# Two MoE layers: rounds of experts in another order, and the weight ring planned in that order of use

## What is computed

```python
def moe(h2, router_w, router_b, w1, w3, w2):
    scores = sigmoid(h2 @ router_w)                    # 256 tokens x 16 experts
    # best of 4 groups by biased scores, then the best 2 experts in it
    gates = sel / sum(sel)
    ...
    for each expert e, xb = the tokens that chose it:
        y = (silu(xb @ w1[e]) * (xb @ w3[e])) @ w2[e]  # 1024 -> 512 -> 1024
        out[tokens] += y * gate
```

## Time and profile before

| what | value |
|---|---|
| median of three runs | 1976.16 us |
| the profiled execution: its own time | 1980.94 us |
| its span, from first to last instruction | 1979.1 us |
| mean granted clock of TensorE | 0.943 of full |
| PE busy | 1756.6 us (89%) |
| DVE busy | 975.3 us (49%) |
| ACT busy | 634.8 us (32%) |
| moved from memory | 427.42 MB |
| MoE 0, from its first expert load by count to its last landing | 245.6 to 480.9 us |
| MoE 1, the same | 639.7 to 877.7 us |

### The profile page before, as it was taken

How to read it: one execution, slowest core, us unless ns; L and a number is a source line. 1 busy time by engine, 2 the same in 40 slices (tenths; PEclk the granted TensorE clock), 3 DMA queues, 4 the chain that set the end, 5 groups by cost and what they waited for, 6 DMA issues and landing times.

```text
span 1979.1 us, 23273 instructions
## 1 busy us (share of the span) xinstructions
PE 1756.6 (89%) x9412; PEld 1218.6 (62%) x9412; DVE 975.3 (49%) x1773; ACT 634.8 (32%) x1079; POOL 94.8 (5%) x136
## 2 busy tenths in 40 slices
PE   6998889976898899769988879999999798889997
PEld 5655644432676444327545658888888574579997
DVE  5673410001444100026377556888766756766665
ACT  2154111111141111113256435322222425654443
POOL 0780000000000000000000000000000100000000
PEclk9989889988999899889979999999999898989999
DMA  9979199999854999992200012354544121025530
GB/s 390 381 283 364 42 404 421 421 421 421 368 207 177 403 421 416 422 421 111 85 22 1 22 64 86 149 202 181 207 176 191 43 107 43 1 88 189 174 146 22
DMA packets 61861, 430.09 MB, mean 217 GB/s; under 512 B 6576, under 2 KB 9776, under 8 KB 9904
## 3 DMA queue, kind: packets, MB, share of 16 engines
q1 hardware_dynamic: 61744, 428.49, 54.3%
HBM read 427.42 MB, written 1.05 MB: 216 GB/s over the span
## 4 chain that ended last, share of the span: by engine, by line
PE 58%; DVE 17%; DMA 13%; ACT 7%; SPq 2%; issue 2%; DVEq 0%; ACTq 0%
PE bank L293 13%; PE bank L297 10%; PE bank L299 9%; PE bank L298 9%; DMA work<-in_ws_dram 9%; PE bank L1090 6%; DMA ring<-in_ws_dram 4%; DVE ring_halves L2356 2%; SPq L2714 2%; PE bank L332 2%; ACT work_halves L2350 2%; PE bank L2029 1%; PE bank L2006 1%; DVE work L439 1%; PE bank L2380 1%
## 5 line engine op out<-in xcount | busy, mean ns | idle before, releaser
L297 PE MATMUL bank<-work_halves 128*128 128x512 f32 (+1 forms) x1344 | 472.3, 351 | 29.0 <-DVE HH_halves L2648 15.0
L299 PE MATMUL bank<-work_halves,ring_halves 128*128 128x512 f32 (+1 forms) x1344 | 461.1, 343 | 0.0
L297 PEld LDWEIGHTS bank<-work_halves 128*128 128x128 f32 x1344 | 258.5, 192 | 66.3 <-DVE HH_halves L2648 16.2
L298 PE MATMUL bank<-HH_halves,work_halves 128*128 128x512 f32 (+1 forms) x832 | 289.3, 348 | 0.0
L1090 PE MATMUL bank<-ring,work 128*32 128x512 f32 (+2 forms) x872 | 249.1, 660 | 34.0 <-DMA work<-in_ws_dram 17.3
L299 PEld LDWEIGHTS bank<-work_halves,ring_halves 128*128 128x128 f32 x1344 | 258.4, 192 | 28.9
L1090 PE MATMUL bank<-work 128*32 128x512 f32 (+2 forms) x664 | 214.0, 647 | 30.2 <-DMA ring<-in_ws_dram 17.3
L2356 DVE TENSOR_TENSOR ring_halves<-ring,work_halves 128x2048 fp32r<-128x2048 f32 x72 | 164.7, 2288 | 51.0 <-ACT work_halves L2350 51.0
L298 PEld LDWEIGHTS bank<-HH_halves,work_halves 128*128 128x128 f32 x832 | 161.6, 194 | 20.4 <-issue 2.2
L298 PE MATMUL bank<-work_halves 128*128 128x512 f32 (+1 forms) x512 | 172.0, 336 | 0.0
L1341 DVE TENSOR_TENSOR work<-work,bank 128x512 f32<-128x512 f32 x14 | 9.6, 688 | 296.2 <-PE bank L1090 296.2
(11 more groups left out here) (319 smaller groups left out, 2305.1 us busy)
## 6 DMA issues: line engine op xcount, KB each, us to landing
ring<-in_ws_dram SPq DMA_DIRECT2D x285, 1024.0 KB, 9.9
work<-in_ws_dram SPq DMA_DIRECT2D x119, 1024.0 KB, 22.8
con<-in_con_dram SPq DMA_DIRECT2D x1, 1192.0 KB, 27.5
XX<-in_xT_dram SPq DMA_DIRECT2D x1, 1024.0 KB, 9.8
XX<-in_cT_dram SPq DMA_DIRECT2D x1, 1024.0 KB, 27.0
out_dram<-XX SPq DMA_DIRECT2D x2, 512.0 KB, 3.2
par<-in_par_dram SPq DMA_DIRECT2D x1, 338.0 KB, 3.2
con<-in_con_dram SPq DMA_DIRECT2D x1, 128.0 KB, 3.0
```

The source lines that it names most:

```text
L297: pe.matmul(out, l[0], r[0], start=start, stop=False)
L298: pe.matmul(out, l[0], r[1], start=False, stop=False)
L299: return pe.matmul(out, l[1], r[0], start=False, stop=stop)
```

## The change

`ROUNDS` has the same seven rounds in another order: first the four of places 8 to 11, then expert 0 alone, then the four of places 12 to 15, then place 1 alone, then the three pairs. The six chunks of expert 0 are planned ahead of all other expert chunks of the layer, and each is taken out of the rotation of slots as it is planned. Its slot comes back to the right end of the deque at the point in `self.w` at which the chunk would have stood. The wait for "rows by count" moves to the first chunk of what is now round 0 (again expert 8).

```diff
-ROUNDS = ((0,), (8, 9, 10, 11), (1,), (2, 3), (4, 5), (6, 7), (12, 13, 14, 15))
+ROUNDS = ((8, 9, 10, 11), (0,), (12, 13, 14, 15), (1,), (2, 3), (4, 5), (6, 7))
...
                 for i in (*self.steps[1], *self.steps[2]):
                     bg.plan(i)
+                fixed = [key for key in self.w if key[2] == 0]
+                for key in fixed:
+                    chunk(self.st, *key)
+                    slots.pop()
                 for key in self.w:
-                    chunk(self.st, *key)
+                    if key in fixed:
+                        slots.append(slot_of[key])
+                    else:
+                        chunk(self.st, *key)
                 slots.remove(WIDE)
...
-            if moe.st.real and key == ("w1", key[1], ROUNDS[1][0], 0):
+            if moe.st.real and key == ("w1", key[1], ROUNDS[0][0], 0):
```

## The result

The changed kernel took 1967.58 us (median of 9 runs, 1962.94 to 1972.34). The kernel before, run beside it, took 1979.96 us (9 runs). The ratio is 0.9942, with a 95% interval of 0.9928 to 0.9957: 11.5 us faster (0.58% of 1979.96; the two medians lie 12.4 us apart), where 14.1 had been forecast. The absolute time that was forecast, 1962, was counted from the 1976.16 of the three runs known then; the nine put the kernel before 3.8 us higher. The profiled execution took 1967.75 us (span 1966.0) against 1980.94.

A forecast was written before the change was run, and what follows sets the result against it. The landing of the weight stream was taken to bound both MoEs; 9.94 + 3.0 + 1.2 = 14.1 us gained, from 1976.16 to 1962 us, range 1956 to 1972, the forecast itself given 62%.

The forecast's parts named there:

- Part 1: Expert 0's two w2 chunks load in the idle ahead of the wait: 4.97 us per MoE, 9.94 us together.
- Part 2: Dips of the stream, one in each MoE, go, with a 0.5 us gap left in MoE 1: 3.0 us gained.
- the turn: Handing back a group's slots in the short ring takes 8.2 us, under the 9.94 us allowed, so no gap.
- Its own test for part 2: A stream over 3 us longer than 90 x 2.485 us from its start would show the dips term wrong.
- Part 3: Middle of the MoE, expert 0 through the pairs: 1.6 us of lag lie on 14 slots again and cost nothing.
- Part 4: Ends of the MoEs, now on a pair: 1.2 us gained in MoE 0, nothing in MoE 1, where win5 lands later.
- (a): Rival: first handing back at low clock, stream dry in both MoEs; 9.0 us gained, 1967 us; 18%.
- (b): Rival: the short ring runs dry at every group, with a turn of 11.9 us against 9.94; 1990 us; 6%.
- (c): Rival: PE is behind on the pairs at the end, so the gain does not pass on; 1971 us; 6%.
- (e): Rival: the change doesn't prefetch at all, which would need the two slots busy; given no chance of its own.
- The clock rule: Matmul bursts shorter than the wait before them begin at low clock: groups of four take 6.31 us, the sum unchanged.

The follow-up runs named there:

- new_order_none: The changed kernel with nothing of expert 0 planned ahead: 96 chunks behind the wait, 14 slots; ratio to the kernel before 1.0056.
- new_order_four: The changed kernel with only expert 0's four w1 and w3 chunks planned ahead: 92 chunks behind the wait, ten slots; ratio to the kernel before 0.9967.
- half_twice: The changed kernel with each first-half group of w1 and w3 in rounds 0 and 2 multiplied twice; ratio to the kernel before 0.9964.
- warm5: The changed kernel with five matmuls on constants ahead of the second, third and fourth groups of rounds 0 and 2; ratio to the kernel before 0.9935.
- four_last_warm5: The changed kernel with its second round of four moved last and five constant matmuls per pause in round 0 only; 1973.82 us, ratio 0.9970.

## Why the prediction was right, and which step was wrong

**Part 1 held.** The loads were ahead of the wait (210 GB/s in a window that had 0), no wait was added, and behind it 90 chunks remain. The stream from start to last landing is shorter by 4.62 and 4.95 us, forecast 4.97. The price of a chunk is shown by new_order_none against new_order_four: 10.16 and 9.84 us for four, forecast 9.94.

**Part 2 failed, as a size.** The step that failed is the turn: "it takes 6.31 + 1.9 = 8.2 us. I keep no gap". It left out the time from the last byte to the landing. In MoE 0 the first eight by-count chunks have passed at 248.39 + 8 x 2.485 = 268.27, and the eighth lands at 250.72 + 20.03 = 270.75, 2.48 us later; in MoE 1 the bytes are through at 655.42 and the landing is at 637.80 + 20.11 = 657.91, 2.49 us later. So the turn is 2.5 + 5.3 to 6.3 (group) + 1.9 = 9.7 to 10.7 us, on both sides of 9.94 and not under it.

The 2.5 us are not a fixed cost of a load. The trace has sixteen landing events for each load, one for each share of it. The first by-count load lands 0.7 us behind its bytes by the same count (251.56 against 250.88), and its sixteen shares land within 0.3 us. Of the eighth load twelve shares land from 268.59 to 268.93 and the other four from 270.25 to 270.75. PE waits for the last share. So most of the missing term is a few shares that fall behind as the stream runs on, not time that every load needs. Which DMA engines these are the events don't say.

The old dip went and a row of small ones came: 413 and 409 GB/s over 50 us. For the same stretch around its dip, before had:

```profile
250.00:300.00 50.00, 43.40 (x248) 22.88 (x249) 4.94 (x13) 10.56 (x20) 0.00 (x0) 0.90 0.99 406
650.00:700.00 50.00, 49.31 (x262) 25.53 (x262) 4.25 (x11) 10.55 (x21) 0.00 (x0) 0.95 0.98 403
```

By these windows the new dips lose 1.1 and 1.5 us where the old lost 1.9 and 2.3; by the lengths of the stream they lose as much as the old, and by the packets they lose 1.1 us less in both MoEs together. In every count it is at most 1.6 us in place of 3.0. A part of the miss lies on the side of before: the prediction read each old dip from one window of 3.5 us, 1.48 and 2.07 us. half_twice shows that the turn stands at its limit, and warm5 and new_order_four that either a faster group or a longer ring takes the dips away.

The prediction could have seen it in its own rows. Its stream in MoE 0 ran from 247.32 to 480.88, 233.56 us. 92 chunks are 228.62 and the dip 1.48; the 3.46 us that are left over stood in no part of the sum. By the packets 2.7 of them are the last landing, and the rest is the dip, which lost more than 1.48. Its own test for part 2 (a stream longer than 90 x 2.485 = 223.65 us by over 3 us) has come true: 228.94, 5.3 over. But it was a poor test, since it left the landing out as well: before lies 4.9 over its 92 chunks by the same count.

The Trainium skill (DMA: Bandwidth & Descriptors, "Anatomy of one DMA — SWDGE (gpsimd) path") puts most of a transfer's fixed cost of about 2 us behind its last byte. These loads come from SP's queue and not by that path, and here the trace doesn't agree: the first load's last share came 0.7 us behind its bytes, and the 2.5 us of the eighth are mostly the distance between its shares (2.2 us from the first to the last).

**Part 3 held.** Behind the first 50 us the windows of 50 us stand at 421 GB/s, but for one of 417 in each MoE (before had one such, in MoE 1), and with eight slots in the rounds of four the pairs did not hold up the stream: PE is busy for all 50 us of 400:450 while the stream stays full. That the order mattered there was seen only in the variants: take the second round of four out from between, and the middle dips to 404.

**Part 4 held.** Forecast 1.2 us in MoE 0 and nothing in MoE 1; the end went from 5.57 to 3.8 us behind the last landing, 1.8 us, and in MoE 1 the landing of win5 sets the end as before. The pair's groups ran at full clock (7.18 us for two).

The terms close in MoE 0: two chunks 4.97, less 0.35 for the dips and the later last landing taken together and 0.3 for a later start (3.66 us from the row by count to the stream, 3.35 before), and 1.8 for the end, make 6.1 (measured 6.07). In MoE 1: 4.95 and some 0.15 for the start and the cut make 5.1 (measured 5.12). The forecast came within its range since the term that failed was 3.0 of 14.1 us, and since the end of MoE 0 gave 0.6 us more than its 1.2.

**The rivals.** (a) put the loss into the first handing back at low clock. That group ran at full clock in both MoEs (the next load went out 3.7 us behind the last fill), and the stream is at 426 GB/s in the window of 260 to 270 us; in MoE 0 it is the second, third and fourth groups, behind waits of 5.42, 4.01 and 3.44 us, that were slow. (b) had the right place, every group of the rounds of four, and the right threshold of 9.94 us, but a turn of 11.9 where it is at most 10.7: not slower than before, and 3 us less gained. (c) did not happen in this order; a loss of that kind shows in the middle of four_last_warm5. (e): the loads did go ahead.

The clock rule that the prediction took from the Trainium skill (TensorE: Matmul & The Clock Gate, "HAM oscillation — how this bites in real kernels") said that bursts shorter than the wait ahead of them begin slow. The trace agrees in part. At full clock a group takes 3.65 us. The three groups behind waits of 5.42, 4.01 and 5.54 us began slow. But one behind 2.99 us (MoE 1, at 667.94) began slow as well, and the one at 290.74, behind 3.44 us, began at full clock and fell to the low one: 5.34 us. Groups of 5.28, 5.34 and 6.25 us ran at a granted clock of 0.69, 0.68 and 0.58. The prediction weighed this price at nothing, because 8.2 was under 9.94. At 10.7 it is not, and it is worth the 0.9 to 1.6 us per MoE that warm5 brought back in its two profiles.

## What to carry to other kernels

Loads moved ahead of a late wait are worth their transfer time only if what remains of the ring still turns in time: count the turn from the last byte of a set, over its landing, its work and the next issue, to the first byte of the next, and hold it against the landing time of the other sets. Take the time to the landing from a load in the middle of the stream and not from the first one: here it grew from 0.7 to 2.5 us within eight loads. Then add up the stream from its first byte to its last landing; what is left over beyond chunks and dips is a term that the forecast does not know yet. A slow engine in front of a stream costs nothing until that turn is reached, and then everything beyond it.

## What was unexpected of the hardware

The landing of a 1 MB load with the queue full came 2.48 and 2.49 us after its bytes had passed, by the count of the stream's rate, and 0.7 us after for the first load. The difference is in its sixteen shares: all within 0.33 us for the first load, while for the eighth four come 1.3 to 1.9 us behind the other twelve, in both MoEs (251.26 to 251.56 and 268.59 to 270.75; 638.35 to 638.68 and 655.75 to 657.90). The stream stood at full rate, by its count, 1.6 us behind the first issue (246.81 to 248.39, 633.93 to 635.54). Five matmuls on constants in each pause raised the granted clock of a stretch of 50 us from 0.79 to 0.94 and brought a group of 32 matmuls from 5.28 to 3.68 us. And PE's pause within its fills of MoE 1, put down to issue alone, was 3.50 us with five matmuls and 2.24 us with four, one profile each, and absent in warm5; its cause was not tried further.
